# A hybrid mixer's causal attention issued between dense blocks, with its gates kept in SBUF and every convolution tap on VectorE

## What is computed

```python
def hybrid_mixer(u, w_in, b_f, w_attn_out, conv_w, conv_b, g_conv, w_conv_out, w_out):
    z = u @ w_in
    q, k, v = z[..., Q0:K0], z[..., K0:V0], z[..., V0:F0]      # 8 heads of 64
    f_logit = z[..., F0:C0] + b_f
    y_attn = forgetting_attention(q, k, v, f_logit) @ w_attn_out
    y_conv = conformer_conv(z[..., C0:GA0], conv_w, conv_b, g_conv) @ w_conv_out
    merged = sigmoid(z[..., GA0:GC0]) * y_attn + sigmoid(z[..., GC0:]) * y_conv
    return merged @ w_out

# forgetting_attention: causal softmax(q k / 8 + c[t] - c[s]) v, c = cumsum(log_sigmoid(f_logit)), by blocks of 128 queries
# conformer_conv: GLU -> causal depthwise convolution of 31 taps + bias -> RMSNorm -> silu
```

## Time and profile before

| | |
|---|---|
| median of 3 executions | 3746.31 us (3745.95 to 3746.52) |
| the profiled execution | 3746.58 us, its span 3743.7 us |
| mean granted TensorE clock | 0.924 |
| TensorE busy | 3457.2 us, 92% of the span |
| VectorE busy | 1953.2 us, 52% |
| ScalarE busy | 1157.2 us, 31% |
| GpSimd busy | 409.6 us, 11% |

### The profile page before, as it was taken

How to read it: one execution, slowest core, us unless ns; L and a number is a source line. 1 busy time by engine, 2 the same in 40 slices (tenths; PEclk the granted TensorE clock), 3 DMA queues, 4 the chain that set the end, 5 groups by cost and what they waited for, 6 DMA issues and landing times.

```text
span 3743.7 us, 38934 instructions
## 1 busy us (share of the span) xinstructions
PE 3457.2 (92%) x15522; PEld 2692.4 (72%) x15522; DVE 1953.2 (52%) x2718; ACT 1157.2 (31%) x1634; POOL 409.6 (11%) x289
## 2 busy tenths in 40 slices
PE   5877888888999999996899999999999789999998
PEld 3655888457888888873378888888887535888886
DVE  6455566435334544478455544564345954454346
ACT  4442111433233322331233322342233123332233
POOL 0233333000000000046000000000001900000000
PEclk7888999699999999996599999999999857999999
DMA  4232000002233232321022232333222201223222
GB/s 170 79 109 95 1 1 10 18 14 84 94 101 96 96 97 95 96 80 40 0 77 96 98 96 96 93 104 100 95 91 87 68 0 46 95 97 101 94 90 75
DMA packets 81891, 288.04 MB, mean 77 GB/s; under 512 B 9392, under 2 KB 11184, under 8 KB 81328
## 3 DMA queue, kind: packets, MB, share of 16 engines
q1 hardware_dynamic: 81712, 285.56, 23.3%
HBM read 283.42 MB, written 2.10 MB: 76 GB/s over the span
## 4 chain that ended last, share of the span: by engine, by line
PE 84%; DVE 10%; issue 3%; ACT 1%; DMA 0%; POOL 0%; SPq 0%; DVEq 0%; ACTq 0%; POOLq 0%
PE PS L1240 67%; DVE CA L2241 3%; PE PS L1526 2%; PE PS L1528 2%; PE PS L1411 1%; PE PS L1400 1%; PE PS L1416 1%; DVE SPL L1845 1%; PE PS L1547 1%; PE PS L1536 1%; PE PS L1470 1%; PE PS L1490 1%; DVE SM L2153 1%; PE PS L1257 1%; PE PS L1478 1%
## 5 line engine op out<-in xcount | busy, mean ns | idle before, releaser
L1240 PE MATMUL PS<-HS,SPL 128*128 128x512 f32 (+1 forms) x7752 | 1794.9, 392 | 18.4 <-DVE HS L1895 11.2
L1240 PEld LDWEIGHTS PS<-HS,SPL 128*128 128x128 f32 (+1 forms) x7752 | 1454.7, 188 | 345.7 <-issue 19.7
L1845 DVE TENSOR_TENSOR SPL<-RAW,SPL 128x1024 fp32r<-128x1024 f32 (+2 forms) x507 | 616.2, 1220 | 815.9 <-ACT SPL L1580 812.1
L1580 ACT ACTIVATE SPL<-RAW 128x1024 fp32r<-128x1024 f32 (+2 forms) x539 | 550.3, 1030 | 971.8 <-PE PS L1240 936.0
L1240 PE MATMUL PS<-FF,SPL 128*128 128x512 f32 x2880 | 654.6, 389 | 0.0
L1240 PEld LDWEIGHTS PS<-FF,SPL 128*128 128x128 f32 x2880 | 540.7, 188 | 112.1
L2417 POOL MEMSET AP__149<- 128x120 f32 x2 | 0.4, 203 | 2034.5 <-PE PS L1240 2034.5
L2241 DVE SCALAR_TENSOR_TENSOR CA<-AP__149,CW,CA 128x512 f32<-128x512 f32 x180 | 180.3, 1002 | 4.0
L2153 DVE TENSOR_REDUCE SM<-PS 128x1 f32<-128x768 f32 (+2 forms) x96 | 62.1, 646 | 164.5 <-PE PS L1529 114.9
L1688 ACT ACTIVATE PB<-PS,SM 128x768 f32<-128x768 f32 (+2 forms) x96 | 62.6, 652 | 268.0 <-DVE SM L2156 268.0
L1526 PE MATMUL PS<-KK,QQ 64*128 64x128 f32 (+3 forms) x128 | 89.2, 797 | 46.5 <-DVE RH L2285 46.5
(11 more groups left out here) (293 smaller groups left out, 3149.0 us busy)
## 6 DMA issues: line engine op xcount, KB each, us to landing
RAW<-in_w_ff_in SPq DMA_DIRECT2D x176, 512.0 KB, 3.5
RAW<-in_w_in SPq DMA_DIRECT2D x88, 512.0 KB, 3.6
RAW<-in_w_ff_out SPq DMA_DIRECT2D x80, 512.0 KB, 3.5
RAW<-in_w_ff SPq DMA_DIRECT2D x64, 512.0 KB, 3.6
RAW<-in_w_mod SPq DMA_DIRECT2D x48, 512.0 KB, 4.4
...
```

Of the source, the lines that this page charges most:

```text
L1240: m = pe.matmul(o, w[x][:, k, rows], r.T[:, r.k0 + k, y, 0:r.cols], start=r.start and k == 0 and (x, y) == (0, 0), stop=r.stop and k == r. ...
L1580: a.activation(SPL[:, s, 0, 0:n], RAW[:, s, 0:n], AF.Copy).then_inc(w_hi, 1)
L1845: v.tensor_tensor(SPL[:, s, 1, 0:n], RAW[:, s, 0:n], SPL[:, s, 0, 0:n], ALU.subtract).then_inc(w_lo, 1)
```

## The change

1. The attention becomes a generator. It is put into `behind` and its units are issued at the ticks of six dense blocks: the second half of the convolution input (two blocks) and the four blocks of attention gates. A tick brings one unit or two (three units in two ticks), and three taps.
2. The four attention gates are computed there and kept in GA after their sigmoid; the four convolution gates are computed after attn_out and kept in GC. `merge` is cut up: `gate` (PSUM times R, then the sigmoid), `gated` (times attn_out), `merge` (times conv_out, the sum, the two parts of MS).
3. All 124 taps run on VectorE; `conv_pool` is gone. One tap a tick during q, k, v; three from there on; what is left when the gates and attn_out are through stands in one run before the statistics of the convolution.
4. The norm of the convolution (`stats_end`) is issued two groups of 12 matmuls into the first convolution gate, and `conv_output` at the ticks of the second.
5. Scores rotate over two banks instead of four; transposes and values have one each; the dense blocks of this stage have four banks. q and k are interleaved in one buffer, QK, over which AS is written head pair by head pair.

The diff, cut to its core:

```diff
-    AS = sb("AS", [128, 4, 2, 512], F32R, 96)
+    GA = sb("GA", [128, 8, 512], F32, 96)
     CP = sb("CP", [128, 4, 2, 512], F32R, 112)
     MS = sb("MS", [128, 8, 2, 512], F32R, 128)
-    QQ = sb("QQ", [128, 4, 512], F32, 128)
-    KK = sb("KK", [128, 4, 512], F32, 136)
+    QK = sb("QK", [128, 4, 2, 512], F32, 128)
+    AS = sb("AS", [128, 4, 2, 512], F32R, 128)
...
+    pairs = [(0, 1, 2, 3)]
+
     def pair():
-        k = next(k for k in range(turn[0], turn[0] + 4) if not {2 * (k % 4), 2 * (k % 4) + 1} & held)
+        k = next(k for k in range(turn[0], turn[0] + 8)
+                 if k % 4 in pairs[0] and not {2 * (k % 4), 2 * (k % 4) + 1} & held)
...
+        taps = [1]
+
         def conv31(blk):
...
+            for k in range(31):
                 q = Rec()
-                q.blk, q.L, q.k, q.done = blk, L, k, count(s_ca) if k == 30 else None
+                q.blk, q.ready, q.L, q.k, q.done = blk, ap_ready[blk], L, k, count(s_ca) if k == 30 else None
                 if k == 30:
                     ca_ready[blk] = q.done
                 emit("conv_tap", q)
-                yield 1
-
-        for j in range(2):
-            dense(W["w_in_2"][l, 6 + j], 8, HS, hx if j == 0 else None, ev_ga(2 * j))
-        for j in range(2):
+                if k % taps[0] == 0:
+                    yield 1
+
+        def conv_half(j, ready):
+            dense(W["w_in_2"][l, 6 + j], 8, HS, ready, ev_ga(2 * j))
             dense(W["w_in_2"][l, 8 + j], 8, HS, None, ev_gb(2 * j))
-        q = Rec()
-        q.ready, q.L, q.done = ap_ready[3], L, count(s_ca3)
-        ca_ready[3] = q.done
-        emit("conv_pool", q)
-        for blk in range(3):
-            behind.append(conv31(blk))
-        rate[0] = 2
+            aside.append(conv31(2 * j))
+            aside.append(conv31(2 * j + 1))
+
+        conv_half(0, hx)
+        rate[0] = 1
...
-            use = take(u % 4)
+            use = take(u % 2)
...
-            s.use, s.p, s.after = take(4 + u % 2), p_ready[u], pt_after[s.h % 2]
+            s.use, s.p, s.after = take(2), p_ready[u], pt_after[s.h % 2]
...
-            s.h0, s.use, s.mark, s.v = h0, take(6 + (h0 // 2) % 2), mark, v_ready[-1]
+            s.h0, s.use, s.mark, s.v = h0, take(3), mark, v_ready[-1]
...
-            if u < 32:
-                f_scores(u)
-                tick(2)
-            else:
-                scale_rows()
-            whole = (units[u - 4][0] - 1, m) if 4 <= u < 36 and (u - 4) % 8 == 7 else None
+        def attention():
+            whole, m = None, None
+            for u in range(37):
+                if whole:
+                    f_values(*whole)
+                if 4 <= u < 36:
+                    m = f_turn(u - 4)
+                if u < 32:
+                    f_scores(u)
+                else:
+                    scale_rows()
+                whole = (units[u - 4][0] - 1, m) if 4 <= u < 36 and (u - 4) % 8 == 7 else None
+                if u % 3:
+                    yield 1
+
+        ga_ready, gc_ready, ms_ready = [None] * 8, [None] * 8, [None] * 8
+
+        def ev_gate(T, j, ready):
+            def ev(i, u):
+                q = Rec()
+                q.use, q.dst, q.sig = u, T[:, 2 * j + i, :], count(s_gsig)
+                emit("gate", q)
+                give(u)
+                ready[2 * j + i] = q.sig
+            return ev
+
+        behind.append(attention())
+        pairs[0], taps[0] = (2, 3), 3
+        conv_half(1, None)
+        for j in range(4):
+            dense(W["w_in_2"][l, 10 + j], 8, HS, None, ev_gate(GA, j, ga_ready))
+        while behind:
+            tick()
+        pairs[0] = (0, 1, 2, 3)
...
+        def ev_attn(j):
+            def ev(i, u):
+                q = Rec()
+                q.use, q.k, q.sig = u, 2 * j + i, ga_ready[2 * j + i]
+                emit("gated", q)
+                give(u)
+            return ev
+
+        for j in range(4):
+            dense(W["w_attn_out_2"][l, j], 4, AS, as_ready if j == 0 else None, ev_attn(j))
...
+        while aside:
+            tick()
+        for j in range(4):
+            mst = stats_add(CA[:, j, :], ACC[:, :], ca_ready[j], j == 0)
+        m_cv = stats_end(mst, RCV[:, :], ACC[:, :], width=512, after=2)
...
+        def conv_output():
+            for j in range(4):
+                q = Rec()
+                q.j, q.rms, q.waits = j, m_cv, [as_ready[3]]
+                q.slot, q.after = tmp()
+                q.scaled, q.silu, q.hi, q.lo = count(s_cn), count(s_cs), count(s_cphi), count(s_cplo)
+                slot_end[q.slot] = cp_ready[j] = q.lo
+                emit("conv_out", q)
+                yield 1
+
+        for j in range(4):
+            h_last = dense(W["w_in_2"][l, 14 + j], 8, HS, None, ev_gate(GC, j, gc_ready))
+            if j == 0:
+                behind.append(conv_output())
         catch_up()
...
-            dense(W["w_attn_out_2"][l, j], 4, AS, as_ready if j == 0 else None, keep(0), at=0)
-            dense(W["w_in_2"][l, 10 + j], 8, HS, None, ev_gate(0, j), at=2)
-            dense(W["w_conv_out_2"][l, j], 4, CP, cp_ready if j == 0 else None, keep(1), at=4)
-            h_last = dense(W["w_in_2"][l, 14 + j], 8, HS, None, ev_gate(1, j), at=6)
+            dense(W["w_conv_out_2"][l, j], 4, CP, cp_ready if j == 0 else None, ev_conv(j))
...
+            v.wait_ge(*r.use.mark)
+            v.tensor_tensor(r.dst, PS[:, r.use.b, :], R[:, :], ALU.mult).then_inc(free[r.use.b], 1)
+
+        def gated(r):
+            t = GA[:, r.k, :]
+            v.wait_ge(*r.sig)
+            v.wait_ge(*r.use.mark)
+            v.tensor_tensor(t, t, PS[:, r.use.b, :], ALU.mult).then_inc(free[r.use.b], 1)
+
         def merge(r):
-            t = MG[:, 2 * r.key + r.i, :]
-            v.wait_ge(*r.after)
+            t = GC[:, r.k, :]
+            v.wait_ge(*r.sig)
             v.wait_ge(*r.use.mark)
-            v.tensor_tensor(t, PS[:, r.use.b, :], R[:, :], ALU.mult).then_inc(free[r.use.b], 1)
-            v.wait_ge(*r.sig)
-            v.wait_ge(*r.y.mark)
-            v.tensor_tensor(t, t, PS[:, r.y.b, :], ALU.mult).then_inc(free[r.y.b], 1)
-            if r.key:
-                v.wait_ge(*r.y.rel)
-                v.tensor_tensor(t, t, MG[:, r.i, :], ALU.add).then_inc(s_merge, 1)
-                v.wait_ge(*r.hi)
-                v.tensor_tensor(MS[:, 2 * r.j + r.i, 1, :], t, MS[:, 2 * r.j + r.i, 0, :],
-                                ALU.subtract).then_inc(s_mslo, 1)
+            v.tensor_tensor(t, t, PS[:, r.use.b, :], ALU.mult).then_inc(free[r.use.b], 1)
+            v.wait_ge(*r.use.rel)
+            v.tensor_tensor(t, t, GA[:, r.k, :], ALU.add).then_inc(s_merge, 1)
...
-        def conv_pool(r):
-            acc = CA[:, 3, :]
-            g.wait_ge(*r.ready)
-            g.wait_ge(*r.L.cw)
-            g.wait_ge(*r.L.pad)
-            g.tensor_scalar(acc, AP_[:, 3, 0:512], CW[:, 93:94], CW[:, 127:128], ALU.mult, ALU.add).then_inc(g_own, 1)
-            own.n += 1
-            for k in range(1, 31):
-                g.wait_ge(g_own, own.n)
-                g.tensor_scalar(PTMP[:, :], AP_[:, 3, k:k + 512], CW[:, 93 + k:94 + k], None,
-                                ALU.mult).then_inc(g_own, 1)
-                own.n += 1
-                g.wait_ge(g_own, own.n)
-                m = g.tensor_tensor(acc, acc, PTMP[:, :], ALU.add)
-                if k < 30:
-                    m.then_inc(g_own, 1)
-                    own.n += 1
-                else:
-                    m.then_inc(s_ca3, 1)
```

More of the change, by code:

```diff
@@ L1059, in f_values @@
             as_ready[h0 // 2] = give(s.use)
-        whole = None
-        for u in range(37):
-            if whole:
-                f_values(*whole)
-            if 4 <= u < 36:
-                m = f_turn(u - 4)
-            if u < 32:
-                f_scores(u)
-                tick(2)
-            else:
-                scale_rows()
-            whole = (units[u - 4][0] - 1, m) if 4 <= u < 36 and (u - 4) % 8 == 7 else None
+        def attention():
[12 more added lines that the diff above has]
+                    yield 1
@@ L1073, in build @@
+        for j in range(4):
+            h_last = dense(W["w_in_2"][l, 14 + j], 8, HS, None, ev_gate(GC, j, gc_ready))
+            if j == 0:
+                behind.append(conv_output())
         catch_up()
         rate[0] = 0
-        for j in range(4):
-            mst = stats_add(CA[:, j, :], ACC[:, :], ca_ready[j], j == 0)
-        m_cv = stats_end(mst, RCV[:, :], ACC[:, :], width=512)
-        cp_ready = []
-        for j in range(4):
-            q = Rec()
-            q.j, q.rms, q.waits = j, m_cv, [as_ready[3]]
-            q.slot, q.after = tmp()
-            q.scaled, q.silu, q.hi, q.lo = count(s_cn), count(s_cs), count(s_cphi), count(s_cplo)
-            slot_end[q.slot] = q.lo
-            emit("conv_out", q)
-            cp_ready.append(q.lo)
@@ L1088, in build, with ev_conv @@
-        ms_ready, hold = [None] * 8, {}
-        def keep(key):
-            def ev(i, u):
-                hold[key, i] = u
```

(20 more changed lines are left out.)

39 lines of the change are left out of this document (18 added, 21 removed).

## The result

The changed kernel takes 3663.37 us (median of 4, 3661.8 to 3665.45) against 3746.41 us before: ratio 0.9779, 95% interval 0.9762 to 0.9796. It is 83 us faster; 150 were forecast. The time lies 8 us above the upper end of the 3555 to 3655 that was given 8 in 10, and 28 above that of the forecast itself (3565 to 3635).

The account below looks back on a forecast made before the run. It took VectorE's queue in q, k, v and TensorE's low clock in attention as limits. Room of 116.0 and 113.9 us less 40 charged gave 76 and 74 per mixer, 150 together: 3596 us, range 3565 to 3635 (64%).

Parts of the forecast that it names:

- the tail: At the convolution's norm, TensorE waits 16.6 us for VectorE's last taps, then 2.5 us cold start: 19 us per mixer.
- the taps: All 124 on VectorE at 0.77 us each without GpSimd, 95.5 us per mixer; VectorE's total hardly moves.
- the table loads: ScalarE changing between exponential and sigmoid: 10 more loads per mixer, 1.28 us each, 13 us, covered by idle time.
- the room of 116: Per mixer, first dense block to first MS product: 420.5 us less 304.5 us of TensorE work at full clock, mixer 0.
- Two of its signs: Expected in the profile after, attention stage: clock 0.9 or more, and no wait over 5 us.
- Lockstep: Attention stage: VectorE and TensorE wait on each other through the scores' banks; 9 us per mixer, bounds 0 and 20.
- first units: The attention's first units wait for QK, RH and the last v in VectorE's queue: 2 us per mixer.
- The clock: Attention stage: 1.00 with short falls where two units follow each other behind a wait; 7 us per mixer, bounds 0 and 33.
- The rival with a mean clock of 0.8: The clock falls in most passes of the interleaved stage, 26 us more per mixer: 3648 us; chance 18%.
- Merges, 3 us: At conv_out, VectorE's work per block outlasts TensorE's and is late by 5 us, 2 of them covered: 3 us per mixer.

Follow-up runs that it names:

- The early RH: The changed kernel with each head's row RH written at the second unit of the head before: 3619.36 us, ratio 0.9663.
- the slow one: The changed kernel with the row RH computed five times over before its release: 3709.64 us, ratio 0.9903.
- the rest is already clean: The changed kernel with a second bank for some transposes and two taps a tick in q, k, v, RH late: 3623.61 us, against RH early as well.
- the best version: The changed kernel with RH early, a second bank for some transposes and two taps a tick in q, k, v: 3559.21 us; again, 3561.7 us.

## Why the prediction was wrong

The sign was right, and so were the tail, the taps and the table loads; two terms, both of the attention stage, came out at two to more than three times their size, and one of them had its mechanism wrong. Per mixer I charged 40 us against the room of 116; the trace after has 72.4 (376.9 - 304.5) in mixer 0. Two of its signs failed with these terms: the stage's clock is 0.85 and not 0.9 or more, and one wait is 5.14 us long where none was to be over 5.

*Lockstep, charged 9 us, and first units, 2.* Measured 23.1 us of idle time (mixer 1: 21.7). This is the step that failed. I sought the coupling between the engines in the bank that the exponential of u-2 frees, a wait that does not occur in the profile after. The coupling is RH, 16.4 us, and I dismissed it with "in a queue that is no longer late". It was in front of me: the earlier trace rows names RH for both first scores they show, and RH is 19.9 of the 26.2 us of idle time in the attention that the prediction counted into its room. It needs no late queue. RH stands behind the last unit's reduce, so most heads wait for it: 1.4 us at the least, and up to 5.2 when taps and evictions stand between. The bound of 20 us, worked out from the bank alone, did not hold either. The early RH removes the waits and 44 us of time, the slow one adds 46. That VectorE has 101 us of work was right (106 measured with the last units), and so was that it is enough for neither engine to be the bound; a percentage of load says nothing on who waits for whom.

*The clock, charged 7 us.* Measured 24 (158.9 us busy at 0.85), inside its bounds of 0 and 33. I had taken its falls to come from the thin units, with a wait only where two of them follow each other. The runs show two causes. With hardly a wait left, 0.95 to 0.96 remain, so the mixture costs some 6 us (140.2 x 0.04), near the 7 that I had charged. The other 18 us come with the waits: 19 us of low clock in both mixers go with RH's waits, 24 when the rest is already clean. Taken away, a wait gave back its length and some two thirds more (24 us of clock for 33 of idle time, 19 for 28); lengthened, it cost 0.4 more (14 for 34). The rival with a mean clock of 0.8 came nearest of those named, but only half of what was missing was clock, and none of them had RH.

*The tail, 19 us.* Right: a wait of 14.3 us where 16.6 were worked out, and 2.8 us behind it (168 matmuls in 41.0 us, 38.2 at the pitch of the earlier trace rows) for 2.5 of cold start. Moving 24 taps to q, k, v takes 12 us of the wait away. The prediction priced it rightly and did not ask how cheaply it could be had: one number, 31 us of the kernel.

*Taps and q, k, v.* Right: 750 ns, no idle time in q, k, v. The rule of the Trainium skill (SBUF — State Buffer, SBUF: two separate sides) is one port pair under an exclusive lock: a VectorE operation with two SBUF inputs, as a tap is, and a GpSimd operation that reads SBUF keep each other out for the whole instruction. Beside GpSimd's TENSOR_TENSOR the trace agrees, each of the 16 taps ending 0.55 us behind it; beside its TENSOR_SCALAR it agrees in part, since 13 of 31 taps lost nothing and the other 18 lost 0.3 to 0.4 us. The mean of both is the 1200 ns.

*Table loads.* Right that they are covered: some 5 us of the kernel, with intervals that overlap. By the rule to batch activations by set (the Trainium skill, ScalarE: Activation LUTs, Table sets) the change should have suffered; the run without the loads shows no more than those 5 us, and ScalarE had two thirds of the stage free.

*Merges, 3 us.* 0.6 measured.

*The rest.* Some 8 us per mixer (72.4 - 23.1 - 24 - 17.1 - 0.6) were under-counted in TensorE's own work: at full clock the stage needs 135 us where I had 132.5, and between thin units a group of 12 dense matmuls takes 2.8 to 2.9 us from start to start for the 2.73 of a long run.

Of the 83 us, 23 are what GpSimd's removal alone gives to the kernel before, and 42 the interleaving (the change against itself with the attention in one piece). The 18 between come from the gates, the norm's place and the order of the rest together; no run took these apart. The split holds in this order of the steps only: in the changed kernel the same removal cost 23 us, by the tail, and in the best version it is worth nothing. Nor did any run show what the clock's 0.04 in the best version hangs on.
